# A two-layer hybrid attention encoder: when TensorE issues the next pair's scores, ahead of or behind the even unit's transposes

## What is computed

```python
hn = rmsnorm(x, g_pre_mix)
proj = hn @ w_in                      # 1024 -> 3072, split among three mixers
y_dil = dilated_attention(...)        # 6 heads of 64, rotary, (window, dilation) in (128,1),(512,4),(2048,16)
y_na = neighbourhood_attention(...)   # 4 heads of 64, 8 x 16 window on a 64-wide grid, position bias
y_conv = gate_b * conv3(gate_c * h_in)
x = x + rmsnorm(concatenate([y_dil, y_na, y_conv]) @ w_out, g_post_mix)
f = (silu(hf @ w_gate) * (hf @ w_up)) @ w_down      # hf = rmsnorm(x, g_pre_ffn)
x = x + rmsnorm(f, g_post_ffn)
```

## Time and profile before

| what | value |
|---|---|
| median of 3 runs | 2977.84 us (2976.98 to 2978.07) |
| the profiled execution, device time | 2975.31 us |
| its span, first to last instruction | 2973.4 us |
| mean granted TensorE clock | 0.998 |
| busy: PE, DVE, ACT, POOL | 99%, 67%, 41%, 31% of the span |
| attention blocks of layer 0 and layer 1 | from 73.4 to about 540 us, and from 1548.8 to about 2017 us |

### The profile page before, as it was taken

The page is one execution under the profiler, slowest core; times in us unless marked ns, Lnnn a source line. Parts: engine busy times, 40 slices in busy tenths (PEclk is TensorE's granted clock), DMA queues, the critical chain, the costliest instruction groups (busy, mean ns, idle before and its releaser), DMA issues.

```text
span 2973.4 us, 50401 instructions
## 1 busy us (share of the span) xinstructions
PE 2946.1 (99%) x19364; PEld 2789.5 (94%) x19364; DVE 1989.9 (67%) x3695; ACT 1222.3 (41%) x2377; POOL 931.0 (31%) x762
## 2 busy tenths in 40 slices
PE   9999999999999999999999999999999999999998
PEld 8888887999999999999988888879999999999998
DVE  7867756388744447677888777563986444476786
ACT  5433444453422225444554344344534222254342
POOL 1211212765622225001452111137555322350013
PEclk9999999999999999999999999999999999999999
DMA  4111012333222226644531110213232222257345
GB/s 159 43 53 61 22 64 82 117 117 108 89 83 71 72 70 191 215 136 155 182 103 52 51 58 15 102 61 135 91 126 82 70 70 70 89 172 260 96 144 198
DMA packets 153452, 307.54 MB, mean 103 GB/s; under 512 B 16128, under 2 KB 76160, under 8 KB 152960
## 3 DMA queue, kind: packets, MB, share of 16 engines
q1 hardware_dynamic: 148784, 291.74, 29.8%
q10 hardware_dynamic: 4432, 12.58, 1.1%
HBM read 238.73 MB, written 57.67 MB: 100 GB/s over the span
## 4 chain that ended last, share of the span: by engine, by line
PE 91%; DVE 4%; POOL 1%; issue 1%; ACT 1%; DMA 0%; ACTq 0%; SPq 0%; DVEq 0%; POOLq 0%
PE PS L2783 27%; PE PS L2785 26%; PE PS L2784 26%; PE PS L2945 3%; PE PS L2914 3%; PE PS L2929 3%; PE PS L2821 1%; POOL OSS L1349 1%; PE PS L2909 1%; PE PS L2882 1%; DVE ACCUM L2114 0%; PE PS L2954 0%; DMA ACCUM<-xt 0%; PE PS L2828 0%; DVE GL L2198 0%
## 5 line engine op out<-in xcount | busy, mean ns | idle before, releaser
L2783 PE MATMUL PS<-XH,WH 128*128 128x512 f32 (+1 forms) x1152 | 432.4, 375 | 6.5 <-DVE VD L2385 2.8
L2785 PE MATMUL PS<-XH,WL 128*128 128x512 f32 (+1 forms) x1152 | 409.8, 356 | 0.0
L2784 PE MATMUL PS<-XL,WH 128*128 128x512 f32 (+1 forms) x1152 | 407.8, 354 | 0.0
L1377 POOL TENSOR_TENSOR GL<-GR,GH 128x512 fp32r<-128x512 f32 x186 | 251.6, 1366 | 366.6 <-ACT GH L1740 306.4
L2783 PE MATMUL PS<-DHH,DWH 128*128 128x384 f32 (+1 forms) x1056 | 328.3, 311 | 0.0
L2785 PE MATMUL PS<-DHH,DWL 128*128 128x384 f32 (+1 forms) x1056 | 326.6, 309 | 0.0
L2784 PE MATMUL PS<-DHL,DWH 128*128 128x384 f32 (+1 forms) x1056 | 325.8, 309 | 0.0
L2783 PEld LDWEIGHTS PS<-XH,WH 128*128 128x128 f32 x1152 | 217.3, 189 | 57.8 <-issue 21.2
L2785 PEld LDWEIGHTS PS<-XH,WL 128*128 128x128 f32 x1152 | 217.1, 188 | 32.9
L2784 PEld LDWEIGHTS PS<-XL,WH 128*128 128x128 f32 x1152 | 217.9, 189 | 24.4
L2784 PE MATMUL PS<-CL0T,GH 128*128 128x384 f32 x704 | 238.4, 339 | 0.0
(11 more groups left out here) (262 smaller groups left out, 8316.3 us busy)
## 6 DMA issues: line engine op xcount, KB each, us to landing
GR<-w_gu SPq DMA_DIRECT2D x62, 768.0 KB, 4.2
RAW<-w_in SPq DMA_DIRECT2D x48, 512.0 KB, 3.7
DHR<-hidden SPq DMA_DIRECT2D x66, 320.0 KB, 4.5
DWR<-w_down SPq DMA_DIRECT2D x66, 256.0 KB, 3.9
S3B<-w_down SPq DMA_DIRECT2D x66, 256.0 KB, 3.2
GR<-w_gu SPq DMA_DIRECT2D x62, 256.0 KB, 2.8
T3B<-hidden SPq DMA_DIRECT2D x44, 320.0 KB, 3.9
hidden<-S1T SPq DMA_DIRECT2D x44, 192.0 KB, 1.9
```

Source lines behind the costliest of these rows:

```text
L1377: nc.gpsimd.tensor_tensor(GL[v % 2][:, m, :, :], GR[v % 2][:, m, :, :], GH[v % 2][:, m, :, :].bitcast(F32), ALU.subtract).then_inc(s_wlo_r ...
L2783: nc.tensor.matmul(out, wh, xh, start=first, stop=False, skip_group_check=reopened)
L2784: nc.tensor.matmul(out, wh, xl, start=False, stop=False, skip_group_check=reopened)
L2785: return nc.tensor.matmul(out, wl, xh, start=False, stop=last, skip_group_check=reopened)
```

## The change

In the loop over the units, the call of `scores` for the next pair now stands in front of `turn(u)` and not behind it. It concerns the even units 0 to 16, so 9 places in a block and 90 in the program. Nothing is added or removed, and the other engines' programs are unchanged.

```diff
                 for u in range(NU):
                     if u and u % 2 == 0:
                         values(u // 2 - 1)
-                    turn(u)
                     if u % 2 == 0 and u + 2 < NU:
                         scores(u // 2 + 1)
+                    turn(u)
                     fill(u)
                     if b == LAST and u in (NU - 3, NU - 2):
                         pe.wait_ge(s_masked, NU * nb + NU - 1)
```

## The result

| | before | changed |
|---|---|---|
| median, same comparison | 2977.67 us (4 runs, 2976.98 to 2978.07) | 2996.28 us (4 runs, 2994.36 to 2997.53) |
| ratio | | 1.006, 95% interval 1.0048 to 1.0072 |
| profiled execution: device time, span | 2975.31, 2973.4 us | 2997.53, 2995.7 us |

A forecast was written before the change was run, and what follows sets the result against it. PE, busy 99% of the span, was taken to bound the kernel. Lost cover 19, second low copy 0.6 and collisions 4.6 sum to 24.2 us, on 2977.84 giving 3002 us; range 2992 to 3013.

The forecast's parts named there:

- PE bounds, other engines' order is free: Whole kernel: PE busy 99% of the span; its waits add to the time, other engines' savings are worth nothing.
- Nothing to gain from the even turn, nothing to wait for ahead of the scores: Even turns and scores at 90 places: gain 0 from a wait removed, cost 0 from waiting for the masking.
- Time needed behind a turn: Needed between even and odd turn: 2.57 us in dilated units, 1.79 in neighbourhood units, 1.47 in block 4's prompt units.
- Lost cover: Odd turns in blocks 2 to 4 wait for copies and exponential where fill is short: 9.5 us a layer, 19 in both.
- The second low copy in block 2: Masking and earlier output push the odd unit's low copy by 0.4, past its short fill: 0.6 us in all.
- Collisions: Blocks 0 and 1: shifted DVE steps meet POOL's weight copies; 2.3 us a layer, 4.6 in both.
- the two held steps: DVE steps held by POOL's copy make PE wait: 1.5 us at block 1 unit 8, 0.9 at block 0 unit 0.
- The tap: DVE step at block 0 unit 6: taken to start first and run free, 0.1 to 0.2 faster; if held, 2 slower.
- The switch of the array: Getting into and out of the 64-row form around the scores, 90 places: taken as 0, bounds 0 to 50 us gain.
- The prediction's own sign for this: Scores behind the values: the forecast is wrong if they take less than 1.9 us there.
- Distances in the roomy pairs: Blocks 0 and 1, where fill is long: even and odd turns 3.49 us apart, over the 2.57 needed, no wait.
- the rival without collisions: Only the lost cover counts, DVE and POOL do not collide: 2977.8 + 19.6 = 2997 us; chance 20%.

## Why the prediction was right, and where it was off

- *PE bounds, other engines' order is free*: right. Nothing was made up later, 18.8 us in the attention are 18.6 in the end.
- *Nothing to gain from the even turn, nothing to wait for ahead of the scores*: right, no such wait in the trace.
- *Time needed behind a turn*: 2.57, 1.79, 1.47 foreseen, 2.53, 1.82, 1.46 measured. In the dilated units the exponential ended 2.47 behind the turn and not 2.42, and the turn started 0.06 behind it and not 0.15.
- *Lost cover*, 19 us: the 15 places named for each layer are those that wait, but nearly all wait a little less. Between the reciprocals and the odd turn PE loses 0.99 where 1.11 was foreseen (block 2, units 6 and 12), 0.60 where it was 0.65 (block 3), 0.62 where it was 0.66 and 0.36 where it was 0.44 (block 4). Together it is about 17, so 2 us were too much. The reason is the switch again: the part of the way out that the first instruction pays now falls behind the turn's start, and with it into the distance. In block 2 the work between the turns took 1.54 (332.39 to 333.93) and not 1.46, in block 4 1.21 (509.73 to 510.94) and not 1.14.
- *The second low copy in block 2*, 0.6: right. From the odd turn to the values it is 2.45, 2.86, 2.87 and 2.87 where it was 2.39, 2.74, 2.80 and 2.80, 0.3 a layer.
- *Collisions*, 4.6 us: the two held steps measured 5.2 alone (6.0 in the trace). By place 1.0 (0.9 foreseen) and 1.76 (1.5 foreseen, 1.9 as the end). The tap ran free and gave 0.3 a layer, where 0.1 to 0.2 were foreseen. Its place was decided by a tenth of a microsecond, and could have gone the other way.
- *The switch of the array*, taken as 0: this is the term that was mis-sized. "What precedes the scores should not matter" held, but the text let the other side pass: what follows them does matter. It measured 0.04 to 0.06 at each of 90 places, 4 to 5 us of gain, inside the bounds that were given (0 to 50). The trace of before had the durations of the weight loads of the transposes and of the fill (141 and 189 ns), though that they are the reason is not shown. The prediction's own sign for this fired: it called itself wrong if the scores take less than 1.9 us behind the values, and they take 1.82 (198.03 to 199.85 in block 1), of which 0.07 to 0.08 come back behind the turn's start.
- *Distances in the roomy pairs*: 3.58 measured, 3.49 foreseen, for the same reason.

The sum thus closes with two errors of one sign, the switch by 4 to 5 and the cover by 2, and small ones of the other: the held steps, and 0.4 of a late DMA in the trace. There is luck in the number as well. 2996.3 lies next to the 2997 of the rival without collisions, and yet the collisions were there: had only the median been read, the wrong mechanism would have seemed the right one.

## What to carry to other kernels

Before work is moved ahead on the engine that bounds, look at what it covers where it stands: between two steps that hand a buffer to other engines, the distance must stay over the time these engines need, and that time can be read from any place where nobody waits. Decide it place by place, since the same reordering gains 0.05 us a pair where the fill is long and costs 0.5 on average where it is short (15.7 over 30 places). And a shift of one engine by two microseconds changes which POOL instruction a DVE step meets, which is worth a look at both timelines for every long step.

## What the runs showed of the hardware

- Leaving the 64-row form costs less when an identity transpose comes first than when a full matmul does: 0.15 against 0.20 us beyond the steps of the instructions themselves (253.30 to 253.79 in the changed kernel, 199.62 to 200.28 in the kernel before). Getting in costs the same behind transposes and behind values: the first scores start 0.10 late.
- DVE steps with two operands in SBUF and POOL's copy exclude each other in both directions: a tap of 1.55 took 3.46 when POOL's copy was 0.28 ahead, and POOL's copy of 2.39 took 3.71 when the tap was 0.11 ahead. In between a series of DVE steps POOL gets in: the first rotary step ran free, the second was held (2.63).
- In the profiled execution of the changed kernel the granted clock was 0.57 from 641 to 645 us, mostly the lower level, though PE had been busy without a gap before it (637 to 641, at 1.00) and was in it. It was 0.57 again from 1484 to 1492, where PE had been busy for 3.29 of the 4.00 us before. What brought it down no run here shows.
